# Which of two engines subtracts: GpSimd gives 97 of its 119 weight splits to VectorE

## The reference

```python
act = jax.nn.gelu(jnp.einsum('chkd,cd->chk', u[idx], xt))
coef = (g * act.astype(jnp.float32)).astype(xt.dtype)
return jnp.einsum('chk,chkd->cd', coef, v[idx])
```

## Time and profile before

| | |
|---|---|
| median of 3 runs | 2171.76 us (2169.7 to 2175.67) |
| the profiled execution: its own time | 2176.31 us |
| its span in the profile | 2175.0 us |
| TensorE matmul busy, weight load busy | 2114.8 us (97%), 2016.3 us (93%) |
| VectorE busy | 1617.3 us (74%) |
| ScalarE busy | 1195.5 us (55%) |
| GpSimd busy | 568.9 us (26%) |
| lo parts on VectorE | 546, 691.8 us, 1270 ns each |
| lo parts on GpSimd | 119, 325.2 us, 2733 ns each |

### The profile page before, as it was taken

The page is one execution under the profiler, slowest core; times in us unless marked ns, Lnnn a source line. Parts: engine busy times, 40 slices in busy tenths (PEclk is TensorE's granted clock), DMA queues, the critical chain, the costliest instruction groups (busy, mean ns, idle before and its releaser), DMA issues.

```text
span 2175.0 us, 41590 instructions
## 1 busy us (share of the span) xinstructions
PE 2114.8 (97%) x17080; PEld 2016.3 (93%) x17080; DVE 1617.3 (74%) x2603; ACT 1195.5 (55%) x2106; POOL 568.9 (26%) x386
## 2 busy tenths in 40 slices
PE   9999999999999999999999999989999999999997
PEld 8898999999999988888889998979999999899997
DVE  7887767899998499965567657968656764788664
ACT  6776566455434444445557755855455544566553
POOL 7422244233222233233333002242001101113001
PEclk9999999999999999999999999999999999999999
DMA  5443455555444555455545554224554555544553
GB/s 171 155 131 101 148 173 169 185 176 192 156 162 159 175 165 164 157 192 194 194 165 185 186 194 136 69 80 155 192 194 147 189 189 194 178 134 157 192 194 117
DMA packets 101131, 357.15 MB, mean 164 GB/s; under 512 B 12048, under 2 KB 15440, under 8 KB 100816
## 3 DMA queue, kind: packets, MB, share of 16 engines
q1 hardware_dynamic: 100080, 352.35, 49.5%
q10 hardware_dynamic: 864, 2.16, 0.3%
HBM read 352.86 MB, written 1.05 MB: 163 GB/s over the span
## 4 chain that ended last, share of the span: by engine, by line
PE 75%; DVE 14%; ACT 4%; issue 2%; DMA 2%; POOL 2%; SPq 0%; POOLq 0%; ACTq 0%; DVEq 0%
PE PS L325 75%; DVE wlo L413 4%; DMA raw<-stream 2%; DVE w L2792 1%; ACT dgh L333 1%; ACT whi L333 1%; DVE H L2725 1%; DVE bn L2676 1%; DVE H L2723 1%; DVE act L1767 1%; DVE ohA L1885 1%; DVE act L1810 1%; POOL wlo L413 0%; POOL R L1288 0%; DVE act L1818 0%
## 5 line engine op out<-in xcount | busy, mean ns | idle before, releaser
L413 DVE TENSOR_TENSOR wlo<-raw,whi 128x1024 fp32r<-128x1024 f32 x546 | 691.8, 1270 | 207.7 <-ACT whi L333 206.9
L333 ACT ACTIVATE whi<-raw 128x1024 fp32r<-128x1024 f32 (+1 forms) x667 | 699.0, 1050 | 180.4 <-PE PS L325 96.2
L325 PE MATMUL PS<-bn,whi 128*128 128x256 f32 x3328 | 594.5, 281 | 15.1 <-DVE bn L2676 5.0
L325 PEld LDWEIGHTS PS<-bn,whi 128*128 128x128 f32 x3328 | 509.2, 188 | 21.1 <-issue 10.2
L325 PE MATMUL PS<-n,whi 128*128 128x256 f32 (+1 forms) x2784 | 510.6, 285 | 4.5 <-DVE wlo L410 3.1
L413 POOL TENSOR_TENSOR wlo<-raw,whi 128x1024 fp32r<-128x1024 f32 x119 | 325.2, 2733 | 676.3 <-ACT whi L333 676.2
L325 PE MATMUL PS<-bn,wlo 128*128 128x256 f32 x1664 | 458.3, 279 | 0.0
L325 PEld LDWEIGHTS PS<-n,whi 128*128 128x128 f32 x2784 | 429.5, 189 | 9.0 <-issue 3.9
L325 PE MATMUL PS<-n,wlo 128*128 128x256 f32 (+1 forms) x1392 | 391.7, 281 | 0.0
L325 PE MATMUL PS<-whi,c 128*128 128x512 f32 x1024 | 324.4, 393 | 0.6 <-ACT act L333 0.6
L325 PEld LDWEIGHTS PS<-bn,wlo 128*128 128x128 f32 x1664 | 311.9, 187 | 0.0
(11 more groups left out here) (355 smaller groups left out, 2918.9 us busy)
## 6 DMA issues: line engine op xcount, KB each, us to landing
raw<-stream SPq DMA_DIRECT2D x666, 512.0 KB, 3.3
abias<-c_alibi ACTq DMA_DIRECT2D x1, 1536.0 KB, 6.7
H<-xt SPq DMA_DIRECT2D x4, 256.0 KB, 6.4
out<-H SPq DMA_DIRECT2D x3, 256.0 KB, 2.2
mask<-c_mask SPq DMA_DIRECT2D x1, 272.0 KB, 6.6
K<-Vh SPq DMA_DIRECT2D x2, 136.0 KB, 4.5
K<-Vl SPq DMA_DIRECT2D x2, 136.0 KB, 5.3
out<-H ACTq DMA_DIRECT2D x2, 128.0 KB, 1.9
```

The source lines that it names most:

```text
L325: return self.nc.tensor.matmul(out, l, r, start=start, stop=stop, skip_group_check=True)
L333: return self.nc.scalar.activation(out, in_, func, **kw)
L413: k.s[q].inc(me.e.tensor_tensor(lo[:, :], raw[:, :], hi[:, :].bitcast(F32), ALU.subtract))
```

## The change

`lo_by_pool(s)` gets a new condition. `PLAN.at["u", 0]` is tile 720, slab 90, and `PLAN.at["u", NKEY // 2]` is tile 1232, slab 154.

```diff
 def lo_by_pool(s):
 
-    return (10 <= s <= 18 and s % 2 == 0) or (21 <= s <= 345 and s % 3 == 0) or (417 <= s <= 431 and s % 3 == 0)
+    return PLAN.at["u", 0] <= SLAB * s < PLAN.at["u", NKEY // 2] and s % 3 == 0
```

## The result

The changed kernel takes 2160.06 us in the median (2152.92 to 2162.0), the kernel before 2175.67 (2169.7 to 2178.76) in the runs beside it; the ratio is 0.9923, with a 95% interval of 0.9905 to 0.9941. That is 0.8% faster, 12.8 to 20.7 us. The forecast was 2159.7 us, but the kernel before is slower than the three runs shown had it: 2174.8 us in the median of 35 runs, not 2171.8. So the change gained about 15 us where the sum of the forecast had 12.1, and the time came out right because the two differences cancel.

A forecast was written before the change was run, and what follows sets the result against it. TensorE was taken to bound nearly all, with VectorE nearly full behind it and fuller in `cin`. Terms 5.2 + 0.8 + 0.7 + 0.6 + 2.0 + 0 + 2.8 = 12.1 us, from 2171.8 to 2159.7 us; range 2153.5 to 2167.

The forecast's parts named there:

- VectorE becomes the bound: Second half of u, first half of v: VectorE needs more time than the stages have; 27 us, 2199 us; chance 0.06.
- the half gain: Only v is won; in block 1 and `cin` other things come due just behind: 5.4 us, 2166.4 us; chance 0.17.
- (a): Block 1, slabs 10 to 18, five moved: TensorE's waits of 5.8 us shrink to 0.6; gain 5.2 us.
- (b): Heads, slabs 21 to 48: the wait for `K` shrinks by 0.8 us and the shorter `PT` wait, 0.7, goes.
- (c): Projections and query columns, slabs 51 to 87: the wait for `o` goes, 0.6 us, bounds -0.5 and 0.6.
- (d): Second half of u and first half of v, slabs 156 to 281: six waits in v go, 2.0 us.
- (e): Second half of v, 21 slabs: VectorE has idle time enough and TensorE no waits; 0.
- (f): `cin`, slabs 417 to 429: VectorE's taps are no longer held, its last tap comes earlier; 2.8 us, bounds 1 and 3.8.
- (g): Loads: SyncE's wait for slab s + 3 moves from GpSimd's subtraction to VectorE's, without TensorE waiting; 0.
- the first half of u: GpSimd keeps its lo parts there with VectorE nearly full; TensorE has no waits to lose or win; counted as nothing.
- the clock rival: Between 177 and 280 us shorter waits keep the clock up: 3 us more won, 15.2 us, 2156.6 us; chance 0.15.

## Why the prediction was right, and where it was not

**The bound and the price.** VectorE's time was the right measure, and a subtraction on GpSimd did cost VectorE 1.6 us. The runs turn that mean over two groups into a count: one held instruction for each, 1.61 or 1.55 us. The rival that VectorE becomes the bound is out, and so is the half gain: v gives 1.9 of the 14.8 us.

**(a) Block 1, 5.2 us.** The stage gives 4.6 in the mean. VectorE's held instructions were read rightly, but the step that sent the wait for `isig` away failed: it is 1.4 us as before. GpSimd's part of that chain did go. ScalarE's last gate waited 0.91 us for an L1309 before the change and follows its predecessor without a gap after it. The row before and the row after, from the two first traces:

```profile
82.99 0.49 ACT L333 ACTIVATE isig<-PS,par 128x272 f32<-128x272 f32 x1 [0.91 <-POOL XC L1309]
...
80.25 0.52 ACT L333 ACTIVATE isig<-PS,par 128x272 f32<-128x272 f32 x1
```

So it is in all 13 traces: idle for 0.90 to 0.94 us in the four with GpSimd in the stage, not at all in the nine others. What TensorE waits for now is ScalarE itself, which from 75.12 us on, when VectorE's L1063 is through, makes twelve activations in a row, two `whi` of 1.07 us among them. The prediction had followed the chain through GpSimd and not looked at what ScalarE had still to do. L1309 meets the same conflict in the other direction, beside a `wlo` that VectorE began at 77.67 us and beside none, but ScalarE doesn't wait for it here:

```profile
78.09 1.44 POOL L1309 TENSOR_TENSOR XC<-XC,isig 128x272 f32<-128x272 f32 x1 [0.29 <-ACT isig L333]
...
73.91 0.88 POOL L1309 TENSOR_TENSOR XC<-XC,isig 128x272 f32<-128x272 f32 x1 [4.85 <-ACT isig L333]
```

The wait that is left was to be 0.6 us and is 2.4. In the pair of first traces that makes 2.7 to 3.1 us. That it is 4.6 on average comes for the most part from a cost the forecast didn't have: of the four traces with GpSimd in block 1, three have a stretch of 3.4 or 6.8 us at 1.2 GHz between 60 and 90 us, of the nine others none has. The first trace, from which the term was read, is the fourth, and 1.1 us quicker than the mean of the four. The other 0.4 us are the changed kernel's first trace, slower by that than the mean of its seven. So the size of (a) came out nearer than its waits do, which fell by 3.4 us.

**(b) and (c), 2.1 us.** The stage gives 4.7. `K` (0.86), the shorter `PT` (0.7) and `o` (0.6) went as worked out. Mis-sized was (c): beside `o` there is a wait for `n` of 1.2 to 1.5 us in three of the four traces, and it goes too. In the first trace it is only 0.3 us, because TensorE itself was slow there, at 1.2 GHz for 3.4 us from 226 us on, and so late for `n`. This wait was hidden under a slow clock, and I took the row at its word. Together these are 3.5 us. Of the other 1.2 some 0.6 are clock (all four traces with GpSimd have 6.8 us at 1.2 GHz in this stage, three of the nine without have 3.4); the rest isn't assigned. The bounds for (c), -0.5 to 0.6, were bounds for one trace.

**(d) 2.0 us, (e) 0.** Measured 1.9 and 0 in these stages. VectorE at 140 of 152 us: 140.5 and 141.5. Not seen was what goes with the same edit 400 us later, the shorter wait for `bsq`.

**(f) `cin`, 2.8 us.** Measured 3.6, within the bounds. The train of taps came 3.4 us closer, and the wait for the sum shrank from 4.2 to 3.5 us, where the forecast had it staying. Of the two waits inside the stage one stayed, at 1.6 us.

**(g) and the first half of u, 0.** No wait for a load appeared in PEER. The wait for L1818 is 1.3 us instead of 0.5; the rule there is the same, only the times at which GpSimd's subtractions meet VectorE's steps have shifted.

**The clock.** It was a rival with 0.15, and a part of it may have come. The granted clock of each run, averaged, is 0.9916 over 58 runs of the kernel before and 0.9932 over 13 of the changed one. A run's time x (1 - clock) is 18.2 us and 14.8 in the mean, so at most 3.4 of the 15.5 us between the means are clock. It can't all be: a stretch at 1.2 GHz costs nothing where TensorE has nothing to do, and in every trace the last 6.4 to 9.5 us at that level lie behind the last matmul. In a line through the 58 runs of the kernel before, 1 us more of this product goes with only 0.4 us more of time, which would make it about 1.5 us here. That at least 12.1 us remain for work and waits has the forecast's number by chance, since its terms are off one by one. The clock didn't come mainly from where the rival had it: in 177:280 it reads 0.97 in the first traces of both kernels, and over all 13 that stage gives 0.6 us; it came in part from 60:90, as above. Which wait starts which stretch isn't shown.

**The base.** That 2159.7 was met all the same is luck. What cancelled the miss is the 2171.76 us, a median of three, 3.0 below that of 35. The forecast took it as it stood, though the profiled execution lay 4.5 us above it. Against 2174.8 the forecast's sum gives 2162.7, and the clock rival's 15.2 us 2159.6, which is what was measured, though not from the rival's source alone.

## What to carry to other kernels

An elementwise instruction on GpSimd with two SBUF operands isn't free for VectorE: it holds the next instruction of VectorE that has two SBUF inputs and comes due while it runs until about its own end. So compare its duration with what VectorE would need itself, and move work to GpSimd only where VectorE has idle time in front of its next such instruction, or where GpSimd's instruction reads nothing from SBUF; with one operand it held VectorE for the first 0.7 us of 2.13. When a wait goes with an engine's work, look at what the engine behind it in the chain has still to do: here ScalarE stood right behind GpSimd. Read the size of small waits from several executions: in one trace of four the clock had fallen just where a wait of 1.3 us would have been seen.

## What the runs showed of the hardware

How long GpSimd holds VectorE goes with how much it reads and not with how long it runs: on 128x768, two operands held for 1.33 us of 1.47, one operand for 0.68 us of 2.13, a fill of 0.74 us not at all (one shape, one trace of each).

TensorE's pace in the first feed-forward part of block 2 has two levels at the same granted clock of 1.00. In 1200:1280, of the changed kernel and of the one without lo parts on GpSimd:

```profile
1200.00:1280.00 80.00, 80.00 (x682) 80.00 (x680) 49.16 (x67) 55.41 (x113) 2.45 (x2) 1.00 0.58 191
```

```profile
1200.00:1280.00 80.00, 80.00 (x709) 80.00 (x708) 48.77 (x64) 55.54 (x110) 3.78 (x4) 1.00 0.62 198
```

682 against 709 matmuls begin in the same 80 us, 117 and 113 ns each, with 191 and 198 GB/s moved. The whole stage, matmuls 8800 to 10400, takes 193.7 or 195.3 to 195.4 us in eleven traces and 187.2 in two (this one and the one with two reads on GpSimd, whose runs of 2152.4 and 2152.9 us are among the fastest). The changed kernel has a run of 2152.9 us too, but neither of its two traces has the faster level. That the level belongs to the execution and not to the kernel is likely, since the programs of these stages are the same, but no kernel was traced at both; what sets it wasn't found.
